# One layer of a hybrid diffusion backbone: first norm's sums in columns, low parts of attention ahead of the sinks, first units ordered by heads

## What is computed

```python
hx = modulate(rms_norm(x, norm1_w), sh1, sc1)        # y * (1 + scale) + shift, per channel
rx, rgx, qx, kx, vx, gax, gbx = split_cols(hx @ w_in)
# recurrent branch: decay of each channel
log_a = -LRU_C * r * softplus(-lam)
# windowed attention, 8 heads, 2 key heads, blocks of 128 queries
s = q @ [keys of 3 neighbouring blocks, context keys]
m = max(s.max(-1), sink)
p = exp(s - m);  denom = p.sum(-1) + exp(sink - m)
o = (p @ values) / denom
# then: gated merge, output projection, second norm, gated ConvFFN, final norm
```

## Time and profile before

| | |
|---|---|
| three executions | 1819.81, 1822.35, 1822.40 us; median 1822.35 |
| the profiled execution | 1821.91 us, of which 1820.1 are its span |
| mean granted TensorE clock | 0.988 of full speed |
| TensorE matmuls busy | 1744.0 us (96% of the span) |
| VectorE busy | 1217.9 us (67%) |
| ScalarE busy | 697.5 us (38%) |
| GpSimd busy | 560.6 us (31%) |
| DMA | 178.44 MB, mean 98 GB/s |

### The profile page before, as it was taken

How to read it: one execution, slowest core, us unless ns; L and a number is a source line. 1 busy time by engine, 2 the same in 40 slices (tenths; PEclk the granted TensorE clock), 3 DMA queues, 4 the chain that set the end, 5 groups by cost and what they waited for, 6 DMA issues and landing times.

```text
span 1820.1 us, 22774 instructions
## 1 busy us (share of the span) xinstructions
PE 1744.0 (96%) x8176; PEld 1450.3 (80%) x8176; DVE 1217.9 (67%) x1382; ACT 697.5 (38%) x900; POOL 560.6 (31%) x264
## 2 busy tenths in 40 slices
PE   3999999999999889999999999999999999999997
PEld 1897888888788778878888868888888888888886
DVE  7987666668515487878315469999998988514423
ACT  4235555567201178760002135444444444202202
POOL 2035676666345375635456720000000000000000
PEclk8999999999999999999999989999999999999999
DMA  9131111111435300037225512222222124523112
GB/s 382 56 102 53 50 50 59 57 49 41 138 120 173 81 1 0 0 120 262 104 69 195 156 66 82 86 87 81 92 81 92 69 87 168 189 99 134 53 47 93
DMA packets 54812, 178.44 MB, mean 98 GB/s; under 512 B 10720, under 2 KB 11104, under 8 KB 54112
## 3 DMA queue, kind: packets, MB, share of 16 engines
q1 hardware_dynamic: 45632, 148.78, 23.2%
q10 hardware_dynamic: 9120, 28.84, 4.8%
HBM read 141.42 MB, written 30.93 MB: 95 GB/s over the span
## 4 chain that ended last, share of the span: by engine, by line
PE 78%; DVE 12%; DMA 4%; issue 3%; ACT 1%; POOL 1%; SPq 0%; DVEq 0%; ACTq 0%; POOLq 0%
PE acc L877 15%; PE acc L879 15%; PE acc L878 15%; PE gp L877 10%; PE gp L879 10%; PE gp L878 10%; DVE pt_lo L2218 1%; DVE prob L2168 1%; DMA wg<-in_mod_rest 1%; DVE wg L2256 1%; DVE wgr L2256 1%; PE acc L1151 1%; DMA wst<-in_w_in 1%; DMA wgr<-in_mod_rest 1%; DVE hx_lo L2119 1%
## 5 line engine op out<-in xcount | busy, mean ns | idle before, releaser
L877 PE MATMUL acc<-hx_hi,whi_both 128*128 128x512 f32 x672 | 263.8, 393 | 17.7 <-DVE hx_lo L1954 14.9
L878 PE MATMUL acc<-hx_lo,whi_both 128*128 128x512 f32 x672 | 262.5, 391 | 0.0
L879 PE MATMUL acc<-hx_hi,wlo_both 128*128 128x512 f32 x672 | 262.2, 390 | 0.0
L703 POOL TENSOR_TENSOR whi_both<-wst,ones 128x1024 fp32r<-128x1024 f32 x58 | 157.8, 2721 | 262.4 <-PE acc L879 230.8
L705 POOL TENSOR_TENSOR wlo_both<-wst,whi_both 128x1024 fp32r<-128x1024 f32 x58 | 175.8, 3032 | 4.5
L877 PEld LDWEIGHTS acc<-hx_hi,whi_both 128*128 128x128 f32 x672 | 126.7, 189 | 47.6 <-DVE hx_lo L1954 15.9
L879 PEld LDWEIGHTS acc<-hx_hi,wlo_both 128*128 128x128 f32 x672 | 126.6, 188 | 26.8
L878 PEld LDWEIGHTS acc<-hx_lo,whi_both 128*128 128x128 f32 x672 | 126.8, 189 | 25.3
L877 PE MATMUL acc<-T_hi,fac_hi 128*128 128x512 f32 x264 | 102.8, 389 | 0.3 <-DVE fac_lo L2429 0.3
L879 PE MATMUL acc<-T_hi,fac_lo 128*128 128x512 f32 x264 | 102.7, 389 | 0.0
L878 PE MATMUL acc<-T_lo,fac_hi 128*128 128x512 f32 x264 | 102.7, 389 | 0.0
(11 more groups left out here) (359 smaller groups left out, 4590.7 us busy)
## 6 DMA issues: line engine op xcount, KB each, us to landing
wst<-in_w_in SPq DMA_DIRECT2D x43, 512.0 KB, 3.4
wst<-in_w_up SPq DMA_DIRECT2D x26, 512.0 KB, 3.9
wg<-in_mod_rest ACTq DMA_DIRECT2D x24, 512.0 KB, 5.2
ffn_row_scratch<-ca SPq DMA_DIRECT2D x24, 512.0 KB, 2.6
wst<-in_w_down SPq DMA_DIRECT2D x32, 384.0 KB, 3.1
g_in<-ffn_row_scratch SPq DMA_DIRECT2D x24, 512.0 KB, 7.5
wup<-in_w_up SPq DMA_DIRECT2D x22, 512.0 KB, 3.8
wmod<-in_mod_first SPq DMA_DIRECT2D x16, 512.0 KB, 15.2
```

The costliest lines, as they stand in the source:

```text
L703: nc.gpsimd.tensor_tensor(whi[s][:, 0:kc, :], wst[s][:, 0:kc, :], ones_of(kc), mult).then_inc(S["w_hi"], 1)
L877: mm(out_ap, w_h, x_h, start=first, stop=False)
L878: mm(out_ap, w_h, x_l, start=False, stop=False)
L879: return mm(out_ap, w_l, x_h, start=False, stop=last)
```

## The change

It does the following.

- First norm: squares are added one behind the other (seven additions) instead of in four pairs; PE sums them into eight columns of `acc[1]`, ACT takes the root of 128x8 values, DVE the reciprocal and two sets of diagonals (`xdiag`, 128x512 each), PE spreads these into `acc[0]`. `scaled(0)` reads the spread values in PSUM; ACT copies them to `rstd_x` behind the high part of row 0, for the other rows. ACT splits the first two weights ahead of the root, not behind it.
- `ident` is loaded behind the fifth x row instead of behind the wait for `kw_ready`.
- POOL's first low part waits for the diagonals (`rstd_done` 3).
- The softplus series moves from the start of DVE's program to behind `add_swapped_key(1)`; ACT's first decay waits for it.
- Units 1 and 2 change places: (0,0), (1,0), (0,1), (1,1). The twofold tiles are chosen by u for the first and last units (`side`), by kh in the loop.
- PE makes scores 0 and 1 of unit 0 ahead of query row 7, scores 2 and 3 behind it; the four maxima of unit 0 stand inside the last pair of rotations, two before the last row is rotated and two within.
- In every unit DVE makes low blocks 3 and 4 of the unit before ahead of `sinks`.

```diff
             step(0, 0, 0, None)
-            step(0, 1, 1, (0, 0, 0))
-            step(1, 0, 2, (0, 1, 1))
-            step(1, 1, 3, (1, 0, 2))
+            step(1, 0, 1, (0, 0, 0))
+            step(0, 1, 2, (1, 0, 1))
+            step(1, 1, 3, (0, 1, 2))
...
+        def side(kh, u):
+
+            return u % 2 if isinstance(u, int) else kh
+
         def block_base(n, u):
 
-            if not isinstance(n, int) or 0 < n < XT - 1:
-                return 5 * u - 2
-            return 4 * u if n == 0 else 5 * (2 * n) - 2 + 4 * (u - 2 * n)
+            if isinstance(u, int) and u < 4:
+                return (0, 4, 9, 13)[u]
+            return 5 * u - 2 if not is_edge(n) else 5 * (2 * n) - 2 + 4 * (u - 2 * n)
 
...
             for k in range(KC):
                 sp.dma_start(xraw[:, k, :], D["x_rows"][k]).then_inc(x_loaded[k], 16)
+                if k == KQ:
+                    sp.dma_start(ident[:, :], D["ident"]).then_inc(S["late_loaded"], 16)
...
             sp.wait_ge(S["kw_ready"], N_KV)
             load_mod(KC - 1)
-            sp.dma_start(ident[:, :], D["ident"]).then_inc(S["late_loaded"], 16)
...
+            pool.wait_ge(S["rstd_done"], 3)
...
-            for k in range(KC // 2):
-                pe.wait_ge(S["sq_pair"], k + 1)
-                for h in range(2):
-                    last = mm(acc[0][:, HALF * h:HALF * (h + 1)], ones[:, :], xsq[:, 2 * k + 1, HALF * h:HALF * (h + 1)],
-                              start=k == 0, stop=k == KC // 2 - 1)
+            pe.wait_ge(S["sq_pair"], KC - 1)
+            for m in range(XT):
+                last = mm(acc[1][:, 2 * m:2 * m + 2], xsq[:, KC - 1, P * m:P * (m + 1)], ones[:, 0:2], start=True, stop=True)
+            last.then_inc(S["sq_columns"], 1)
+            for h in range(2):
+                pe.wait_ge(S["rstd_done"], h + 2)
+                last = mm(acc[0][:, HALF * h:HALF * (h + 1)], ones[:, :],
+                          xdiag[:, 4 * h:4 * h + 4, :].rearrange("p t n -> p (t n)"), start=True, stop=True)
             last.then_inc(S["acc_full"], 1)
 
             def first_part(k, o):
...
-            with pe.Fori(0, KC // 2) as i:
+            with pe.Fori(0, KC // 2 - 1) as i:
                 product(A_Q, W_Q, hx_hi, hx_lo, per=2, i=i)
                 product(A_Q + 1, W_Q + 1, hx_hi, hx_lo, per=2, i=i)
-
-
-
-            pe.wait_ge(S["k_lo_s"], 1)
-            pe.wait_ge(S["vc_s"], 2)
...
             def attention(n, kh, u, before):
-                score(n, kh, u, 0)
-                score(n, kh, u, 1)
                 if before:
+                    score(n, kh, u, 0)
+                    score(n, kh, u, 1)
                     for j in range(3):
                         flip(*before, j)
...
+            pe.wait_ge(S["k_lo_s"], 1)
+            score(0, 0, 0, 0)
+            score(0, 0, 0, 1)
+            product(A_Q + 7, W_Q + 7, hx_hi, hx_lo)
+            pe.wait_ge(S["vc_s"], 2)
             units(pe, attention, lambda n, kh, u: ([flip(n, kh, u, j) for j in range(3)], flip_and_weigh(n, kh, u)))
...
-            full(act, 0)
-            for h in range(2):
-                part = slice(HALF * h, HALF * (h + 1))
-                ins = act_of(rstd_x[:, part], acc[0][:, part], ACT.Sqrt, scale=1.0 / D_MODEL, bias=epsc[:, 0:1])
-                ins.then_inc(S["x_root"] if h == 0 else acc_read[0], 1)
+            act_of(rms[:, 8:9], epsc[:, 0:1], ACT.Sqrt)
             high_w(0)
             high_w(1)
+            act.wait_ge(S["sq_columns"], 1)
+            act_of(rms[:, 0:XT], acc[1][:, 0:2 * XT:2], ACT.Sqrt, scale=1.0 / D_MODEL, bias=epsc[:, 0:1]).then_inc(S["x_root"], 1)
...
+                if k == 0:
+                    act_of(rstd_x[:, :], acc[0][:, :], ACT.Copy).then_inc(acc_read[0], 1)
...
                     act.wait_ge(S["y_done"], 2 * c)
+                else:
+                    act.wait_ge(S["lru_w"], 2)
...
             def scaled(k):
                 dve.wait_ge(S["mod_ready"], k + 1)
-                v.scalar_tensor_tensor(out=xraw[:, k, :], in0=xraw[:, k, :], scalar=mod[:, 0, 1, k:k + 1], in1=rstd_x[:, :],
+                if k == 0:
+                    full(dve, 0)
+                else:
+                    dve.wait_ge(acc_read[0], 1)
+                v.scalar_tensor_tensor(out=xraw[:, k, :], in0=xraw[:, k, :], scalar=mod[:, 0, 1, k:k + 1],
+                                       in1=rstd_x[:, :] if k else acc[0][:, :],
                                        op0=mult, op1=mult).then_inc(S["xs_done"], 1)
 
...
-            def pair_squares(j):
-                dve.wait_ge(S["sq_done"], 2 * j + 2)
-                v.tensor_tensor(xsq[:, 2 * j + 1, :], xsq[:, 2 * j + 1, :], xsq[:, 2 * j, :], add).then_inc(S["sq_pair"], 1)
-
             silu_row(0)
-            pair_squares(0)
-            pair_squares(1)
             silu_row(1)
-            pair_squares(2)
-            pair_squares(3)
+            for k in range(1, KC):
+                dve.wait_ge(S["sq_done"], k + 1)
+                if k > 1:
+                    dve.wait_ge(S["sq_pair"], k - 1)
+                v.tensor_tensor(xsq[:, k, :], xsq[:, k, :], xsq[:, k - 1, :], add).then_inc(S["sq_pair"], 1)
             dve.wait_ge(S["silu_ready"], 1)
             modulation(0, 0)
+            dve.wait_ge(S["x_root"], 1)
+            v.reciprocal(rstd0[:, 0:XT], rms[:, 0:XT]).then_inc(S["rstd_done"], 1)
+            dve.wait_ge(S["rstd_done"], 1)
+            dve.wait_ge(S["late_loaded"], 16)
             for h in range(2):
-                if h == 0:
-                    dve.wait_ge(S["x_root"], 1)
-                else:
-                    dve.wait_ge(acc_read[0], 1)
-                part = slice(HALF * h, HALF * (h + 1))
-                v.reciprocal(rstd_x[:, part], rstd_x[:, part]).then_inc(S["rstd_done"], 1)
-            dve.wait_ge(S["rstd_done"], 2)
+                v.tensor_tensor(xdiag[:, 4 * h:4 * h + 4, :], ident[:, :].rearrange("p (o n) -> p o n", o=1).to_broadcast([P, 4, P]),
+                                rstd0[:, 4 * h:4 * h + 4].rearrange("p (t o) -> p t o", o=1).to_broadcast([P, 4, P]), mult)\
+                    .then_inc(S["rstd_done"], 1)
             scaled(0)
             for k in range(1, KC):
                 modulation(k, 0, between=k - 1)
...
+            dve.wait_ge(S["lru_e"], 2)
...
+            v.tensor_scalar(decay[:, 1, :], lru[:, 4, :], LRU_C, None, mult).then_inc(S["lru_w"], 1)
...
+                    if meanwhile and s == 1:
+                        meanwhile(0)
...
-                        meanwhile()
+                        meanwhile(2)
...
-            rotate_queries(KC // 2 - 1, lambda: [maxima(0, 0, 0, h) for h in range(2)])
...
+            rotate_queries(KC // 2 - 1, lambda h0: [maxima(0, 0, 0, h) for h in (h0, h0 + 1)])
...
                     maxima(n, kh, u, 1)
                 if before:
                     low_block(*before, 0)
-                maxima(n, kh, u, 2)
-                if before:
+                    maxima(n, kh, u, 2)
                     low_block(*before, 1)
                     low_block(*before, 2)
-                maxima(n, kh, u, 3)
-                sinks(n, kh, u)
-                if before:
+                    maxima(n, kh, u, 3)
                     low_block(*before, 3)
                     low_block(*before, 4)
+                sinks(n, kh, u)
                 denominators(n, kh, u)
```

More of the change, by code:

```diff
@@ L837, in step @@
             def step(n, kh, u, before):
-                if isinstance(u, int) and u < N_KV:
-                    pool.wait_ge(S["q_rope"], Q_PER_KV * (u + 1))
+                if isinstance(u, int) and u in (0, 2):
+                    pool.wait_ge(S["q_rope"], Q_PER_KV * (kh + 1))
                 split_queries(n, kh, u)
@@ L1633, in sink_exp @@
                 act.wait_ge(S["s_es"], 2 * u + 1)
-                act_of(esink[:, kh, :], esink[:, kh, :], ACT.Exp).then_inc(S["s_es"], 1)
+                act_of(esink[:, side(kh, u), :], esink[:, side(kh, u), :], ACT.Exp).then_inc(S["s_es"], 1)
             def norm_heads(n, kh, u):
@@ L2086, in _ @@
             add_swapped_key(1)
+            dve.wait_ge(S["lru_e"], 2)
+            link(v.tensor_scalar(lru[:, 2, :], lru[:, 1, :], 2.0, None, add))
+            link(v.reciprocal(lru[:, 3, :], lru[:, 2, :]))
+            link(v.tensor_tensor(lru[:, 2, :], lru[:, 1, :], lru[:, 3, :], mult))
+            link(v.tensor_tensor(lru[:, 3, :], lru[:, 2, :], lru[:, 2, :], mult))
+            link(v.tensor_scalar(lru[:, 4, :], lru[:, 3, :], 1.0 / 19, None, mult))
+            for o in (17, 15, 13, 11, 9, 7, 5, 3):
+                link(v.scalar_tensor_tensor(out=lru[:, 4, :], in0=lru[:, 4, :], scalar=1.0 / o, in1=lru[:, 3, :],
+                                            op0=add, op1=mult))
+            link(v.scalar_tensor_tensor(out=lru[:, 5, :], in0=lru[:, 4, :], scalar=1.0, in1=lru[:, 2, :], op0=add, op1=mult))
+            link(v.tensor_scalar(lru[:, 6, :], lru[:, 7, :], 0.0, None, ALU.max))
```

(13 more changed lines are left out.)

64 lines of the change are left out of this document (26 added, 38 removed).

## The result

Median of 6 runs after: 1813.29 us (1809.06 to 1814.79); before, on the same chip: 1822.38 us (6 runs). Ratio 0.9948, 95% interval 0.9935 to 0.996: faster by 9.5 us (7.3 to 11.8). The forecast was 1809.2 with a range of 1804.5 to 1816.5. The profiled execution took 1813.32 us, span 1811.4. The sign and the range held; the gain, 9.5 us, is 3.2 smaller than the 12.7 of the sum.

What follows compares the result with a forecast made beforehand. TensorE, busy for 96% of the span, was taken as the bound, so only its gaps or lower clock could be won. A 4.6 + B 9.1 - C 1.0 = 12.7 us, from 1821.9 to 1809.2 us; range 1804.5 to 1816.5.

Steps and rivals of the forecast that it cites:

- A: First norm, the chain to TensorE's first products: k=1 at 44.0 instead of 48.53, 4.6 us gained; bounds 2.3 and 6.9.
- steps (1) to (6): First norm: additions, column sums, root and diagonals, spreading, row 0 scaling, GpSimd's low parts; TensorE starts near 36.3, not 40.83.
- does that last: After the first norm: TensorE 4.6 us earlier, VectorE 2.3, meeting at the low context part with nothing to spare; 4.6 kept.
- rival (c): The first norm gives only VectorE's 2.3 us: 1811.5 us in total; chance 0.12.
- B: Attention units, low parts ahead of the sinks: 0.72 us per middle unit, 9.1 us gained in sum; bounds 2 and 10.
- rival (a): Attention units: another wait ends last, ScalarE's high parts or late norms; 0.2 us per unit left, 1815.9 us; chance 0.13.
- (d): Attention units: norms fall beside GpSimd's, pushing back the next unit's first maximum; slower, 1826.2 us; chance 0.03.
- C: Start of attention, order of the first units and two early scores: 1.0 us lost; bounds 1.5 gained and 3 lost.
- Clock: Start of attention: no clock drop after the new 1.5 us wait; the two remaining idle stretches end in half clock as now.
- rival (b): The 1.5 us wait before the early scores drops the clock, costing 1.7 us: 1810.9 us; chance 0.12.

Runs made afterwards that it cites:

- experiment 4: Changed kernel with the last two x rows' products taken as all four outputs of row 6, then of row 7: 1810.21 us, ratio 0.9936.
- edit 7: Changed kernel with scores 0 and 1 of unit 0 behind the last query row, order of units kept: 1806.86 us, ratio 0.9918.
- 10: Kernel before with the new order of the first four units and place of the maxima, but no early scores: 1820.38 us, ratio 0.9988.
- 9: Changed kernel with row 7 wanted late and scores 0 and 1 of unit 0 behind the last query row: 1807.62 us, ratio 0.9918.
- 3: Kernel before with only the new order of the first four units, unit 0's maxima moved, and the two early scores: 1823.97 us, ratio 1.001.

## Why the prediction was right, and where it was not

**A, steps (1) to (6).** Column sums to 24.79 (24.4 forecast), first product 35.81 (36.3), k=1 at 43.43 (44.0), row 1 scaled at 39.50 (40.1). The spreading took 3.78 us, 0.95 a pass and near the 1.06 of the earlier trace rows, where I had taken 1.9 for all four; so row 0 was scaled at 30.03 instead of 28.0. The later steps made this good, since GpSimd had VectorE's idle 3.36 us for itself. Scaling from PSUM was not held up by GpSimd: 1.28 us. The softplus chain cost nothing visible.

**A, "does that last": this step failed.** The text had both numbers, "TensorE is 4.6 earlier but VectorE only 2.3", looked for the next handover at the low context part, and kept 4.6. It missed a nearer one: the last two rows are taken by groups of outputs, which asks for row 7 half a period early. There TensorE waited 1.92 us and fell back to VectorE's lead. The trace of experiment 4 shows that this wait did it: without it the lead at 113 is 4.78 instead of 2.85, and the handover that I did look at holds. How much of that reaches the end is less sure, 2.2 us by ratios whose intervals overlap, and no gain was seen beside edit 7. Measured: A is worth 1.3 us (up to 2.9), near rival (c) with its 2.3, and not 4.6.

**B.** 9.8 us measured against 9.1. The term per unit was 0.86 instead of 0.72: I left 0.1 of the wait, and none was left; from the last product ahead of it (started at 717.60) to the one behind it (718.74) it was 1.14 us before and is 0.29 after. In the middle units the norms were no wait, though `esink`'s place left 0.2 us: rival (a) is out, and (d) with it, since `esink` fell to 0.15 and the norm stayed at 0.55.

**C.** The wait of 1.5 us for the first queries came (1.57), and the transposes started at 640.80, which is 1.3 earlier than before with A's 1.4: no gain of its own, as reckoned. Forecast 1.0 lost, measured 1.8. Experiments 7 and 10 show that the sum hid two terms of opposite sign, +2.2 and -4.0.

I had balanced the 2.9 us later query row with 2.9 us of maxima and exponentials beside the swap, and both came about as reckoned: the row's copy started 3.3 us later, and the path behind it was 3.2 shorter. The mistake was to take the second for a fruit of the first. In experiments 7, 9 and 10 the path is 2.6 us shorter with the scores behind the row, so the early scores paid 3.3 us for 0.6. The reading of the path before was wrong too: it didn't go through the norms, which ended at 640.96 (639.59 + 1.37), but through the scores of unit 1, which waited for the same row's queries and ran to 642.10. That the part as a whole came near its forecast was luck: its two halves, a gain and a larger loss, were never priced apart. The transposes came at 640.80 and not near 637.5; of these 3.3 us 3.2 are the lead of A that was gone by then (1.4 at 618 instead of 4.6).

**Clock.** The waits of 1.57 and 1.92 us were followed by no drop, as forecast (the granted clock was 1.00 in 618 to 622 and in 75.5 to 79.5), so rival (b) did not come at its place. But the low clock in this stretch went on until 644.3, where it ended at 642.7 before, although the transposes had started 1.3 us earlier; the prediction took what stood behind the long wait to be "as now". How long it stays low differs between traces whose instructions are equal there (experiments 3 and 9), and one trace can't price it. The Trainium skill (TensorE: Matmul & The Clock Gate, Part 1) also says that the instant of the change differs from run to run; the traces agree.

**The sum.** 12.7 forecast, 9.5 measured: A 3.3 less, B 0.7 more, C 0.8 less; the parts alone give 9.3. The range held because its bounds were wide and B, the largest term, was right; that the misses of B and C cancel is luck.

## What to carry to other kernels

When two engines work in a pipeline, a head start of one is worth only what the other has too: at the first handover where the consumer asks earlier than row by row (here, the last two rows in groups of outputs) it falls to the producer's lead. Split an edit that "moves work into an idle stretch" into its halves and price each: in the kernel before, the order of the units with the place of the maxima was worth 2.2 us, and moving two scores ahead of the last producer cost 4.0, though they seemed to fill a wait. And if a part's gain and its cost come out equal in a sum, look at which chain really ends last there.

## What I had not expected of the hardware

- VectorE operations on one or two columns with SBUF inputs took 2.19 and 2.27 us beside GpSimd's subtraction of two SBUF tiles, against 0.16 each in the changed kernel, where GpSimd stood still (23.55 and 23.75); two diagonals 5.43 against 1.29. The Trainium skill (SBUF — State Buffer, Who interferes with whom) says that a VectorE instruction with two SBUF inputs contends with a GpSimd instruction that reads SBUF, that the port pair they share is an exclusive lock, and that issue order, not op shape, decides who blocks; these rows agree, and GpSimd's two subtractions beside them took 5.02 us. In the changed kernel `hx_lo` (3.23) and the modulation (3.39) show the same.
- How long TensorE stays at 1.2 GHz behind the same wait differs between traces: behind waits of 2.75 and 2.74 us the twelve transposes took 1.50 us in one kernel and 2.79 in another with the same instructions there. Total times of one kernel spread by 2 to 6 us. In the 49 runs of the kernel before, the two with a mean clock of 0.992 took 1819.6 us on average and the four with 0.987 took 1824.0; in between it is less clear (1822.6 with 0.988 and 1822.7 with 0.989).
